# A three-block kernel on one core: two SSD convolutions in a later stage, and the gate sums of the matrix memory in four column groups

## What is computed

```
def lru_mlstm_layer(...):
    x_mc = silu(causal_conv(x_m, conv_m_w, conv_m_b))
    q = einsum('bshi,hij->bshj', xmc_h, w_q)
    k = einsum('bshi,hij->bshj', xmc_h, w_k) * (MLSTM_DQK ** -0.5)
    v = einsum('bshi,hij->bshj', xm_h, w_v)
    gin = concatenate([q, k, v], axis=-1)      # 1024 + 1024 + 2048 features
    gates = gin @ w_if + b_if                  # 8 gates for each token
    ...

def ssd_layer(...):
    z, xbc, dt = split(x @ w_in)
    xbc = silu(causal_conv(xbc, conv_w, conv_b))   # 6144 features, 4 taps
    xs, bm, cm = split(xbc, [4096, 5120])          # 8 groups of heads
    y = ssd_scan(xs, dt, a, bm, cm) + d_skip * xs
    return rmsnorm(y * silu(z), per group) @ w_out
```

## Time and profile before

| | |
|---|---|
| median of 3 runs | 3513.75 us |
| the profiled execution | 3514.01 us, its span 3512.2 us |
| granted TensorE clock, mean | 0.995 |
| busy: TensorE, VectorE, ScalarE, GpSimd | 3472.1, 2230.2, 1602.8, 670.4 us |
| DMA | 626.83 MB, mean 178 GB/s |

### The profile page before, as it was taken

The page is one execution under the profiler, slowest core; times in us unless marked ns, Lnnn a source line. Parts: engine busy times, 40 slices in busy tenths (PEclk is TensorE's granted clock), DMA queues, the critical chain, the costliest instruction groups (busy, mean ns, idle before and its releaser), DMA issues. The chain is left out here.

```text
span 3512.2 us, 44745 instructions
## 1 busy us (share of the span) xinstructions
PE 3472.1 (99%) x18296; PEld 2895.4 (82%) x18296; DVE 2230.2 (63%) x2155; ACT 1602.8 (46%) x1768; POOL 670.4 (19%) x551
## 2 busy tenths in 40 slices
PE   9999999999999999999999999999999999999998
PEld 7777888888887778888888878888888788878887
DVE  5667646464656577656464658966667476865786
ACT  5555433333344565333333345633454444553564
POOL 1221000000000221000000001560000059781560
PEclk9999999999999999999999999999999999999999
DMA  6444555555555354555555554555444455445554
GB/s 225 144 164 168 188 190 184 190 191 185 186 180 191 132 180 157 190 187 186 190 190 183 202 180 162 180 188 185 163 146 154 156 186 199 164 173 185 181 203 150
DMA packets 94783, 626.83 MB, mean 178 GB/s; under 512 B 10928, under 2 KB 13232, under 8 KB 21392
## 3 DMA queue, kind: packets, MB, share of 16 engines
q1 hardware_dynamic: 84096, 601.99, 47.7%
q0 software_dynamic: 3168, 11.41, 1.0%
q10 hardware_dynamic: 7344, 10.94, 1.0%
HBM read 622.13 MB, written 2.16 MB: 178 GB/s over the span
## 5 line engine op out<-in xcount | busy, mean ns | idle before, releaser
L2400 PE MATMUL ps<-act,whi 128*128 128x512 f32 x4384 | 1552.8, 397 | 1.1 <-DVE wlo L1443 1.1
L2402 PE MATMUL ps<-act,wlo 128*128 128x256 f32 x4384 | 1234.6, 282 | 0.0
L1443 DVE TENSOR_TENSOR wlo<-raw,whi 128x2048 fp32r<-128x2048 f32 x402 | 935.5, 2347 | 457.3 <-ACT whi L982 446.4
L2400 PEld LDWEIGHTS ps<-act,whi 128*128 128x128 f32 x4384 | 824.8, 188 | 199.4 <-issue 3.5
L982 ACT ACTIVATE whi<-raw 128x2048 fp32r<-128x2048 f32 x356 | 679.6, 1913 | 614.8 <-DMA raw<-in_w_down 310.4
L2402 PEld LDWEIGHTS ps<-act,wlo 128*128 128x128 f32 x4384 | 823.6, 188 | 0.7
L866 ACT ACTIVATE whi<-raw 128x2048 fp32r<-128x2048 f32 x213 | 406.2, 1912 | 280.2 <-DMA raw<-in_o_w_in 98.2
L1450 DVE TENSOR_TENSOR wlo<-raw,whi 128x2048 fp32r<-128x2048 f32 x167 | 396.3, 2378 | 152.3 <-ACT whi L866 152.3
L2358 PE MATMUL ps<-whi,act 128*128 128x512 f32 x1152 | 455.7, 396 | 0.0
L2359 PE MATMUL ps<-wlo,act 128*128 128x512 f32 x1152 | 455.2, 395 | 0.0
L2360 PE MATMUL ps<-whi,act 128*128 128x512 f32 x1152 | 455.2, 395 | 0.0
(11 more groups left out here) (419 smaller groups left out, 4536.2 us busy)
## 6 DMA issues: line engine op xcount, KB each, us to landing
raw<-in_w_up SPq DMA_DIRECT2D x128, 1024.0 KB, 4.8
raw<-in_w_down SPq DMA_DIRECT2D x128, 1024.0 KB, 4.8
raw<-in_o_w_in SPq DMA_DIRECT2D x80, 1024.0 KB, 4.8
raw<-in_e_w_in SPq DMA_DIRECT2D x64, 1024.0 KB, 4.8
raw<-in_w_in SPq DMA_DIRECT2D x60, 1024.0 KB, 4.8
raw<-in_w_o SPq DMA_DIRECT2D x32, 1024.0 KB, 4.8
raw<-in_e_w_out SPq DMA_DIRECT2D x32, 1024.0 KB, 4.8
raw<-in_o_w_out SPq DMA_DIRECT2D x32, 1024.0 KB, 4.8
```

Source lines behind the costliest of these rows:

```text
L1443: dve.tensor_tensor(wlo[:, slot, :], raw[:, slot, :], whi[:, slot, :].bitcast(F32), ALU.subtract).then_inc(sem("lo_ready"), 1)
L2400: pe.matmul(ps[:, b + f, :], whi[:, slot, w], a[:, kt, :, :].rearrange("p a t -> p (a t)"), start=(kt == 0), stop=False)
L2402: ins = pe.matmul(ps[:, b + f, S:2 * S], wlo[:, slot, w], a[:, kt, 0, :], start=False, stop=(kt == KT - 1))
```

## The change

Pairs 8 and 9 are convolved and gated in the output projection's stage (`ssd_end`), behind all of GpSimd's work of stage 3. Their room is now the place of group 3's x and z tiles, which is free once `gated_y(3)` is done; ScalarE makes their sigmoids behind two of that stage's weight units. `gate_sums` takes the same 128 x 32 weights for all four tiles, and each of the four products writes its own 32 partitions; only the 8 rows that belong to a tile count. VectorE copies the 128 partitions out, and one product with a matrix of ones and zeros (`gate_pick`, made by GpSimd from `ident`) picks and adds the rows that count. `heads_out(0)` goes ahead of one weight unit on VectorE. The diff, cut to its core:

```
         def conv_room(n):
-            at = 2 * (n % 2) + (24 if n < 10 else 8 * (((n - 10) // 2) % 4))
+            if n in (8, 9):
+                t = ssd_tiles(3, n == 8)
+                return t[:, 0:2, :], t[:, 2:4, :]
+            at = 2 * (n % 2) + (24 if n < 8 else 8 * (((n - 10) // 2) % 4))
...
-        CONV_SEQ = [0, 1, 2, 3, 4, 5, 6, 7, 10, 11, 12, 13, 8, 14, 15, 9] + list(range(16, 24))
+        CONV_SEQ = list(range(8)) + list(range(10, 18)) + [8, 9] + list(range(18, 24))
...
-            return conv_past(n - 2 if n < 10 else -1 if n < 16 else n - 8)
+            return conv_past(n - 2 if n < 8 else -1 if n < 16 else n - 10 if n < 18 else n - 8)
...
-                wait(pool, sem("cv_out"), room_past(n))
+                if n in (8, 9):
+                    pool.wait_ge(sem("s_g"), n - 5)
+                else:
+                    wait(pool, sem("cv_out"), room_past(n))
...
+                if s.get("ssd_end"):
+                    for n in (8, 9):
+                        conv_pair(n)
+                        gate_pair(n)
...
                 if s["kind"] == "e_mix":
+                    pool.wait_ge(sem("scanned"), KT)
+                    pool.wait_ge(sem("ident_in"), 16)
+                    own.then(pool.tensor_tensor(gate_pick, ident[:, 0:8], ident[:, 40:48], ALU.add))
+                    own.then(pool.tensor_tensor(gate_pick, gate_pick, ident[:, 80:88], ALU.add))
+                    pool.tensor_tensor(gate_pick, gate_pick, ident[:, 120:128], ALU.add).then_inc(sem("pick_in"), 1)
...
-                    if g in (1, 2):
-                        conv_pair(7 + g)
...
-                    if g in (1, 2):
-                        gate_pair(7 + g)
...
+                        elif s.get("ssd_end") and g in (2, 3):
+                            high_unit(2 * s["G0"] + 2 * g + 2)
+                            conv_sigmoid(6 + g)
+                            high_unit(2 * s["G0"] + 2 * g + 3)
...
-                    if g in (2, 3):
-                        conv_sigmoid(6 + g)
...
+                if g == 4 and i == 0:
+                    dve.wait_ge(sem("cv_out"), conv_past(9))
...
+                        if i == 1:
+                            heads_out(0)
                         low_unit(U + i + 2)
-                        if 1 <= i < 5:
+                        if 2 <= i < 5:
                             heads_out(i - 1)
...
                         if i == 9:
+                            dve.wait_ge(sem("g_parts"), 1)
+                            dve.tensor_copy(osum[:, :], ps[:, 4, 0:S]).then_inc(sem("g_parts_in"), 1)
                             dve.wait_ge(sem("g8"), 1)
...
+                            if a and t == 9:
+                                pe.wait_ge(sem("pick_in"), 1)
+                                pe.wait_ge(sem("g_parts_in"), 1)
+                                pe.matmul(ps[0:8, 4, 0:S], gate_pick, osum[:, :], start=True, stop=True
+                                          ).then_inc(sem("g8"), 1)
...
-                    def gate_sums(tiles, first=False, last=False):
-                        for n, (kt, src) in enumerate(tiles):
-                            ins = pe.matmul(ps[0:8, 4, 0:S], wif[:, 8 * kt:8 * kt + 8], src,
-                                            start=(first and n == 0), stop=(last and n + 1 == len(tiles)))
+                    def gate_sums(kt, tiles, first=False, last=False):
+                        for n, src in enumerate(tiles):
+                            ins = pe.matmul(ps[32 * n:32 * n + 32, 4, 0:S], wif[:, 8 * kt:8 * kt + 32], src,
+                                            start=first, stop=last)
```

More of the change, by code:

```diff
@@ L420, in build @@
         wif = staged[:, 1, 0, :]
+        gate_pick = lru_c[:, 0, 0:2 * M_H]
         up = slice(DH, P)
@@ L871, in conv_sigmoid @@
                 act.wait_ge(sem("cv"), conv_past(n))
-                wait(act, sem("cv_out"), room_past(n))
+                if n not in (8, 9):
+                    wait(act, sem("cv_out"), room_past(n))
                 act.activation(sig, room, ACT.Sigmoid).then_inc(sem("cv_sig"), 1)
@@ L2762, in head_gates @@
                         off = 2 if part == "k" else 0
-                        gate_sums([(8 * (off // 2) + 2 * (h + a) + d, c_mat[:, 4 * (h + a) + off + d, :])
-                                   for a in range(2) for d in range(2)], first=(t == 0))
+                        gate_sums(4 * off + 2 * h, [c_mat[:, 4 * (h + a) + off + d, :] for a in range(2) for d in range(2)],
+                                  first=(t == 0))
                     def value_gates(h):
                         pe.wait_ge(sem("evacuated" if h % 2 else "m_out"), (e_G0 if h % 2 else 0) + 3 + h // 2)
-                        ins = gate_sums([(KT + 4 * h + f, half(h)[:, f, :]) for f in range(4)], last=(h == 3))
+                        ins = gate_sums(KT + 4 * h, [half(h)[:, f, :] for f in range(4)], last=(h == 3))
                         if h == 3:
-                            ins.then_inc(sem("g8"), 1)
+                            ins.then_inc(sem("g_parts"), 1)
                         wait(pe, sem("vtok_in"), h)
```

## The result

The changed kernel takes **3487.39 us** (median of 4 runs, 3486.69 to 3489.28) against 3514.02 for the kernel before in the same session (3513.14 to 3517.35): ratio 0.9923, 95% interval 0.9906 to 0.9941. The forecast was 3485.5 with a range of 3482 to 3494. The profiled execution took 3487.36 us, with a span of 3485.5; its rows follow.

The account below looks back on a forecast made before the run. TensorE, busy 3472.1 of 3512.2 us, was taken to bound the kernel. Terms -17.10 - 10.80 - 1.30 + 0.66 = -28.54 us against 3514.01 gave 3485.5, range 3482 to 3494.

Parts of the forecast that it names:

- Item 1: SSD stages 2 and 3: without pairs 8 and 9 ahead, the stretches around ssd_bases take 1.89 us; gain 17.10 us.
- The rival that the stall moves to the y sum: SSD stages 2 and 3 keep 1.7 us each and the low clock; gain there 12.2, total 3490.4 us; chance 0.09.
- Item 2: Output projection's stage: the moved pairs cost nothing; only ScalarE can reach TensorE, its delay of some 7 us hidden.
- Item 3: Gate sums: eight groups of four products side by side take 0.48 us each instead of 1.83; gain 10.80 us.
- The rival on serial columns: Gate sums: columns do not run side by side as assumed; fully serial 3496.3 us; chance 0.08 including partial overlap.
- the one on the change of shape: Gate sums: each of eight groups pays 0.20 us more in and out, 3.2 us lost, 3488.7 us; chance 0.05.
- half the gain: Gate sums with columns overlapping only partly: 0.96 us a group, sum -24.7, 3489.3 us.
- Item 4: heads_out(0) ahead of a weight unit on VectorE ends before TensorE asks; gain 1.30 us.
- Item 5: The new product with gate_pick costs 0.66 us, 0.20 of it for the change of shape; no wait taken.
- all cases but the last: Faster by more than 0.2%, chance 0.96: all but ScalarE stopping too long in the output projection's stage, chance 0.02.

Follow-up runs that it names:

- e1: The kernel before with only pairs 8 and 9 moved, gate sums and heads_out(0) as before: 3498.9 us, ratio 0.9954.
- e4: The changed kernel with heads_out(0) back behind its weight unit: 3489.66 us.
- e10: The changed kernel with four needless taps on GpSimd ahead of pair 9's convolution: 3489.36 us.
- e3: The changed kernel with pair 8 begun only after norm_y(3) and the two sigmoids one weight group later on ScalarE: 3486.4 us, ratio 0.9915.
- e9: The changed kernel with one needless tap (two multiplications and an addition) on GpSimd ahead of pair 9's convolution: 3489.47 us.
- e5: The changed kernel with the four gate products in two column groups instead of four, part of the sums left out: 3491.27 us.
- e6: The changed kernel with all four gate products, 32 columns wide, in one column group, most weights wrong: 3498.38 us.
- e7: The changed kernel with all four gate products 128 wide on output rows 0 to 127, most weights wrong: 3494.11 us.

## Why the prediction was right, and where it was not

- **Item 1, -17.10 us: right in mechanism and size.** Both stretches take 1.89 us and the SSD stages save 17.14 us in e1, as in e4 and e10 (138.47 each). In the profiled execution of the changed kernel it is 16.52: 0.6 us went at the y sum of stage 1, whose input stage 0 makes, where no pair was moved. The rival that the stall moves to the y sum is true in small: e3 and e9 wait 0.4 us at that of stage 2. In nine traces with both pairs out of the SSD stages these lost 0 to 1.7 us (138.47 to 140.20), never the 4.9 that it priced. The cover is thinner than the 0.6 us that I read: the y sum itself starts at 3368.24, a step before the product at 3368.49, so GpSimd is 0.3 us ahead of it.
- **Item 2, 0 us: wrong, it costs 1.8.** The step that failed is the sentence that TensorE waits for none of the moved work and that "what can reach it is ScalarE". I followed only the semaphores. The pair reaches VectorE without one, by running beside it on the same memory, and does so while VectorE runs norm_y(3), with 0.8 us of cover. e3 shows it by moving the pair by 4.8 us, and seven traces with the pair at the place of the change and at most one tap more lose 1.7 to 2.0 us. The delay on ScalarE was harmless, as forecast (3.96 us of standing at the sigmoid); the unit behind it began 0.9 us behind its pace of 5.5 us and 2.6 us later than before (3178.35 against 3204.14 less 28.4), not some 7, and e9 hides another tap. Pair 9 ended at 3177.78, where I had 3181.1 (3209.5 less 28.4). That estimate was tighter than I wrote: 3209.5 against a limit of 3209.9 leaves 0.4 us, not 1.
- **Item 3, -10.80 us: measured -10.1** (8 x 1.26). The mis-sized term is the 0.48 for a group, taken from two products of 64 columns, which one of their own shape follows; it is 0.57. The single pick product, with an ordinary one behind it, takes 0.53 (2552.83 to 2553.36), so four side by side cost 0.04 more than one. The rival on serial columns is refuted by e5 and e6, the one on the change of shape by e7 and the equal steps around a group before and after: the cost exists, but was paid before. Where I priced half-overlapping columns I wrote "half the gain"; 0.96 a group is twice the cost and leaves 0.87 of the 1.35.
- **Item 4, -1.30: 1.36 to 1.37** (e4). **Item 5, +0.66: 0.62**, without a wait, as taken. Its 0.20 for the shape is a whole step of which 0.12 is an ordinary one; the missing part stands behind the product.
- e_mix as a whole gained 10.24, not 11.44: besides item 3's 0.7, some 0.4 us are missing between the gate groups and 0.1 behind them. Between them the same 48 products take 5.64 us at one time and 5.86 at another, in most of the traces. Why is open.
- **The sum** of the change's own parts is -10.24 - 16.52 + 1.80 = -24.96 us, against the forecast's -28.54. That the profiled executions nevertheless differ by 26.7 is due to the 2.1 us that the first trace of before lost in unedited work, less 0.4 us ahead and behind. The forecast of 3485.5 was 1.9 us off, with errors of 3.6: that it came so near is in part luck. A slip in the chances: all cases but the last add up to 0.98, not 0.96, and the 0.02 for no change belongs to no case of its own.

## What to carry to other kernels

When work is moved to an idle engine, list what the other engines do in that window on the same memory, not only who waits for whom; here a step of VectorE with 0.8 us of cover did not survive a GpSimd convolution beside it, and waiting for the end of that step cost nothing. Before placing work in a periodic stage, compare the engine's busy time with the period: here a stage with 37 us of 51 in use took some 13 more only with a wait, at both places tried. And read a change stretch by stretch against at least two traces of the old kernel, since a single trace here carried 2.1 us that nobody had edited.

## What the runs showed of the hardware

- The same 3.73 us wait of TensorE is followed by 32 transposes in 5.47 or in 6.79 us, from one execution of one kernel to the next; the granted clock in the 4 us from 2787 is 0.50 in the slow case and 0.66 in the other.
- Beside VectorE's work GpSimd's two multiplications on 128 x 256 took anything from 0.93 to 5.94 us; VectorE's four instructions with two inputs took 3.38 us instead of 1.68 beside GpSimd's convolution.
- Float32 products of 8, 32 or 128 columns stream at one pace, 0.42 to 0.46 us for 256 columns of data; what counts is how many queue in the same columns, and the change of shape, 0.31 us for the group shown (0.27 for each of the last four, whose step behind is shorter).
